# Five changes of stage worked in halves of 256 tokens instead of 512

## The reference

```python
h = rms_norm(x) * (1.0 + sc1) + sh1
x = x + g1 * mixer(h)
h = rms_norm(x) * (1.0 + sc2) + sh2
x = x + g2 * conv_ffn(h, ffn_w_up[i], ffn_conv_w[i], ffn_conv_b[i], ffn_w_down[i])
...
return rms_norm(x) * final_norm_g        # end of the first block; the second starts with a norm of this
```

## Time and profile before

| | |
|---|---|
| median of 3 runs | 3052.89 us (3051.44 to 3061.59) |
| profiled execution, its own time | 3053.06 us |
| its span | 3051.2 us |
| PE busy | 2935.6 us, 96% |
| DVE busy | 1805.3 us, 59% |
| ACT busy | 1100.8 us, 36% |
| POOL busy | 408.3 us, 13% |
| mean granted clock of TensorE | 0.976 |

### The profile page before, as it was taken

The page is one execution under the profiler, slowest core; times in us unless marked ns, Lnnn a source line. Parts: engine busy times, 40 slices in busy tenths (PEclk is TensorE's granted clock), DMA queues, the critical chain, the costliest instruction groups (busy, mean ns, idle before and its releaser), DMA issues. The chain is left out here.

```text
span 3051.2 us, 37640 instructions
## 1 busy us (share of the span) xinstructions
PE 2935.6 (96%) x15078; PEld 2445.1 (80%) x15078; DVE 1805.3 (59%) x2518; ACT 1100.8 (36%) x1569; POOL 408.3 (13%) x390
## 2 busy tenths in 40 slices
PE   6999988999999999999999999999999999999999
PEld 5778767788878878888768878888998887778887
DVE  7456546766656566765646697665764437554443
ACT  3233224333332342324324332234553336442322
POOL 0100111686642100001000000000000103100000
PEclk9999999999999999999989999999999999999999
DMA  6444322455648455554414356653563431123332
GB/s 267 146 131 139 111 89 84 148 176 174 227 131 269 157 166 154 157 152 128 128 44 150 112 178 189 196 166 119 170 182 91 147 95 49 35 89 97 97 97 83
DMA packets 123310, 421.00 MB, mean 138 GB/s; under 512 B 21520, under 2 KB 21520, under 8 KB 122368
## 3 DMA queue, kind: packets, MB, share of 16 engines
q1 hardware_dynamic: 102096, 369.67, 38.6%
q0 software_dynamic: 11056, 41.95, 4.1%
q10 hardware_dynamic: 9984, 6.97, 0.7%
HBM read 401.31 MB, written 19.86 MB: 138 GB/s over the span
## 5 line engine op out<-in xcount | busy, mean ns | idle before, releaser
L121 DVE TENSOR_TENSOR wl<-raw,wh 128x1024 fp32r<-128x1024 f32 x506 | 659.0, 1303 | 556.6 <-ACT wh L118 533.0
L112 PE MATMUL bk<-HH,wh 128*128 128x512 f32 x2176 | 863.4, 397 | 22.6 <-DVE HL L133 13.4
L112 PE MATMUL bk<-HL,wh 128*128 128x512 f32 x2176 | 856.4, 394 | 0.0
L112 PE MATMUL bk<-HH,wl 128*128 128x512 f32 x2176 | 855.6, 393 | 0.0
L118 ACT ACTIVATE wh<-raw 128x1024 fp32r<-128x1024 f32 x506 | 531.1, 1051 | 434.1 <-PE bk L112 426.8
L112 PEld LDWEIGHTS bk<-HH,wh 128*128 128x128 f32 x2176 | 415.0, 191 | 116.2 <-DVE HL L133 15.7
L112 PEld LDWEIGHTS bk<-HH,wl 128*128 128x128 f32 x2176 | 414.2, 190 | 88.0
L112 PEld LDWEIGHTS bk<-HL,wh 128*128 128x128 f32 x2176 | 414.7, 191 | 86.5 <-issue 1.0
L124 DVE CUSTOM_DVE_ANT_0 ttr<-ar,cB 128x1024 f32<-128x1024 f32 x240 | 309.1, 1288 | 2.2
L112 PE MATMUL bk<-gh,wh 128*128 128x512 f32 x704 | 275.4, 391 | 6.0 <-DVE glE L121 5.4
L112 PE MATMUL bk<-gh,wl 128*128 128x512 f32 x704 | 274.6, 390 | 0.0
(11 more groups left out here) (301 smaller groups left out, 3869.4 us busy)
## 6 DMA issues: line engine op xcount, KB each, us to landing
raw<-in_wts_dram SPq DMA_DIRECT2D x506, 512.0 KB, 3.6
ar<-in_ada_dram SPq DMA_DIRECT2D x176, 512.0 KB, 4.3
first<-in_ada_dram SPq DMA_DIRECT2D x16, 512.0 KB, 15.3
F_d<-CA POOLq DMA_DIRECT2D x8, 512.0 KB, 5.3
E_d<-stg POOLq DMA_DIRECT2D x16, 256.0 KB, 4.4
M_d<-K_d POOLq DMA_DIRECT2D x8, 512.0 KB, 11.5
EB<-E_d POOLq DMA_DIRECT2D x8, 512.0 KB, 5.9
EB<-M_d POOLq DMA_DIRECT2D x8, 512.0 KB, 7.3
```

The costliest lines, as they stand in the source:

```text
L112: return Nothing() if self.e is None else self.e.matmul(*a, **k)
L121: return Nothing() if self.e is None else self.e.tensor_tensor(*a, **k)
```

## The change

At the five changes of stage the work is done for tokens 0 to 255 and then for tokens 256 to 511.

- The last output tiles before the change (tiles 5 to 7; 4 to 7 behind retention; both products of tile 7 in glu) are made by `gemm_tail`: first the left halves of all of them, then the right halves. All three weight buffers stay in use until the right half of each is through.
- `half_sum` and `half_turn` for the left half are put between right halves of the tail on PE. Their counterparts for the right half are put into the first pair, behind blocks 2 and 6 of its left half (`pair_between`).
- `first_pair` makes the next stage's first two tiles, the left half over all 8 blocks and then the right half.
- DVE, ACT and POOL do their 512-wide operations as two of 256 (`halves_vec`, `halves_act`, `norm_adds`). The splits of the next stage's first two units, which stood among the additions to X before, now stand behind the first reciprocal and behind the first low half.
- At the change of blocks the two roots one after another become one for the even norm, of the sum of both statistics; the root and reciprocal for the first block's own norm come later.
- f1 and f3 read buffers of their own (`HH1`, `HL1`); the loads of the Fourier matrices on POOL's queue, which lie on the same memory, wait for f1's last up product; two points of `KNOTS` move; the exponential of the s5 tables on ACT comes behind the norm of f0.

```diff
+        def first_pair(e, tag, w0, n_out, xh, xl, xw, banks, frees, between):
+
+            u0 = open_units(tag, w0, n_out)
+            for hf in range(2):
+                for k in range(8):
+                    xw(e, k, hf)
+                    c = slice(k * 128, k * 128 + 128)
+                    for m in range(2):
+                        u, b = u0 + m, BK[banks[m]][:, 256 * hf:256 * hf + 256]
+                        if k == 0 and hf == 0:
+                            claim(e, banks[m])
+                            e.wait_ge(*act.of(("hi", u)))
+                            e.wait_ge(*vec.of(("lo", u)))
+                        h, lo = wh[u % NH][:, c], wl[u % NH][:, c]
+                        e.matmul(b, h, xh(k, hf), start=(k == 0), stop=False)
+                        e.matmul(b, h, xl(k, hf), start=False, stop=False)
+                        mm = e.matmul(b, lo, xh(k, hf), start=False, stop=(k == 7))
+                        if k == 7 and hf == 1:
+                            mm.then_inc(*pe.up(("unit", u), (tag, m)))
+                            bank[banks[m]] = frees(m)
+                    between(hf, k)
+            return u0
...
+        def gemm_tail(e, tag, u0, n_out, nk, cut, xh, xl, xw, banks, frees):
+
+            for hf in range(2):
+                n = cut * nk
+                for m in range(cut, n_out):
+                    bi = banks[m % len(banks)]
+                    b = BK[bi][:, 256 * hf:256 * hf + 256]
+                    claim(e, bi)
+                    for k in range(nk):
+                        u, pos = u0 + n // 8, n % 8
+                        n += 1
+                        if hf == 0:
+                            e.wait_ge(*act.of(("hi", u)))
+                            e.wait_ge(*vec.of(("lo", u)))
+                        xw(e, k)
+                        c = slice(pos * 128, pos * 128 + 128)
+                        h, lo = wh[u % NH][:, c], wl[u % NH][:, c]
+                        e.matmul(b, h, xh(k, hf), start=(k == 0), stop=False)
+                        e.matmul(b, h, xl(k, hf), start=False, stop=False)
+                        mm = e.matmul(b, lo, xh(k, hf), start=False, stop=(k == nk - 1))
+                        names = []
+                        if hf == 1 and (pos == 7 or n == n_out * nk):
+                            names.append(("unit", u))
+                        if k == nk - 1:
+                            names.append((tag, m, hf))
+                        if names:
+                            mm.then_inc(*pe.up(*names))
+                        if k < nk - 1:
+                            yield (m, hf, k)
+                    bank[bi] = frees(m, hf)
+                    yield (m, hf)
...
-        KNOTS = ((0, 0), (2, 16), (12, 24), (58, 48), (76, 48), (122, 78), (138, 78), (152, 88), (212, 124), (222, 124), (240, 136), (260, 136), (318, 192), (600, 192))
+        KNOTS = ((0, 0), (2, 16), (12, 24), (58, 48), (76, 48), (122, 78), (138, 78), (150, 88), (160, 88), (212, 124), (222, 124), (240, 136), (260, 136), (318, 192), (600, 192))
...
+        def half_sum(e, n, hf):
+
+            claim(e, 7)
+            w = con("one1024")[:, 0:1]
+            e.wait_ge(*pool.of(("ss", n.tag, 5) + (of_half(hf) if n.cut <= 5 else ())))
+            token_sums(e, 7, n.ssq[:, part(n, hf)], w, True, False, 2 * hf)
+            for j in (6, 7):
+                e.wait_ge(*act.of(squared(n, j, hf)))
+                mm = token_sums(e, 7, n.tm[j % 2][:, part(n, hf)], w, False, j == 7, 2 * hf)
+            mm.then_inc(*pe.up(("ms", n.tag, hf)))
+            bank[7] = (act, ("root", n.tag, hf))
...
+        def half_turn(e, n, hf):
+
+            b = n.banks[hf]
+            claim(e, b)
+            e.wait_ge(*vec.of(("rs", n.tag, hf)))
+            spread(e, b, n.st[:, 2 * hf:2 * hf + 2], 2).then_inc(*pe.up(("turned", n.tag, hf)))
+            bank[b] = (vec, ("xs", n.tag, 7, hf))
...
+        def halves_vec(e, n, added, split_first, split_next, inverse):
+
+            inverse(0)
+            split_first()
+            added(6)
+            norm_scaled(e, n, 0, 0)
+            norm_scaled(e, n, 1, 0)
+            norm_low(e, n, 0, 0)
+            split_next()
+            added(7)
+            for j in range(1, 8):
+                if j < 7:
+                    norm_scaled(e, n, j + 1, 0)
+                norm_low(e, n, j, 0)
+                if j == 4:
+                    inverse(1)
+            norm_scaled(e, n, 0, 1)
+            for j in range(8):
+                if j < 7:
+                    norm_scaled(e, n, j + 1, 1)
+                norm_low(e, n, j, 1)
+
+        def halves_act(e, n, square, split_next, root):
+
+            root(0)
+            square(6)
+            split_next()
+            norm_high(e, n, 0, 0)
+            norm_high(e, n, 1, 0)
+            square(7)
+            for j in range(2, 8):
+                norm_high(e, n, j, 0)
+                if j == 4:
+                    root(1)
+            for j in range(8):
+                norm_high(e, n, j, 1)
+
+        def pair_between(e, sums, turns):
+
+            def between(hf, k):
+                if (hf, k) == (0, 2):
+                    sums(1)
+                if (hf, k) == (0, 6):
+                    turns(1)
+            return between
...
+        def enter_vec(e, n, tag, x_ms, x_part, u):
+
+            need_mod(e, n.ms, n.parts[0])
+            need_mod(e, n.ms, n.parts[1])
+            halves_vec(e, n, lambda m: add_to(e, tag, m, m % 4, X, L, x_ms, x_part, 1), lambda: lo(e, u), lambda: lo(e, u + 1),
+                       lambda hf: half_inverse(e, n, hf))
...
+                if tail:
+                    for at_ in gemm_tail(e, tag, u0, 8, n, 5, lambda k, hf: half(f.gh, k, hf), lambda k, hf: half(f.gl, k, hf), xw, [0, 1, 2, 3],
+                                         lambda m, hf: (vec, ("x", tag, m, hf))):
+                        if at_ == (5, 1):
+                            f.halves.sum(e, 0)
+                        if at_ == (6, 1):
+                            f.halves.turn(e, 0)
...
+        HH1, HL1 = at("HH1", Z + 32768, [P, 8, L], R), at("HL1", Z + 49152, [P, 8, L], R)
+        n_f1 = norm("f1", X, L, HH1, HL1, 1, (3, 4), [], cut=7)
...
+            def inverse(hf):
+                st = n_e.st[:, 2 * hf:2 * hf + 2]
+                e.wait_ge(*pe.of(("ms", "fin", hf)))
+                e.tensor_scalar(st, BK[7][:, 2 * hf:2 * hf + 2], EPS, EPS, ALU.add, ALU.mult).then_inc(*vec.up())
+                e.wait_ge(*vec.now())
+                e.tensor_tensor(st, st, BK[7][:, 4 + 2 * hf:6 + 2 * hf], ALU.add).then_inc(*vec.up(("again", hf)))
+                half_inverse(e, n_e, hf)
...
             fence(e, "s5")
+            e.wait_ge(*pe.of((("f1", "up", NF - 1), 1)))
             e.dma_start(v_x.dl[:, :, :, :], d["dft512"]).then_inc(*d_dl["e"].up("dft"))
```

425 lines of the change are left out of this document (281 added, 144 removed).

## The result

The changed kernel took 3071.8 us (median of 5 runs, 3068.6 to 3079.9), the kernel before 3054.5 us (5 runs, 3051.4 to 3061.6): ratio 1.0052, 95% interval 1.0038 to 1.0066. It is slower, by more than the 0.3% that the prediction took for what a measurement can tell. The forecast was 3060 us with a range of 3046 to 3068: the way was right, slower, but the time lies above the range, on the side that had a chance of 0.39.

What follows compares the result with a forecast made beforehand. PE, busy for 96% of the span, was taken as the bound, with 53.2 us to win at the five changes. 3053.1 + 3.7 (windows) + 3.5 (half clock) = 3060 us, range 3046 to 3068.

Steps and rivals of the forecast that it cites:

- the side that had a chance of 0.39: Whole kernel slower by more than 0.3%, above 3062.0 us; chance 0.39.
- foreseen without clock: Five windows, tail's place to 49th matmul, before any clock term: together 111.3 against 107.57 us, +3.7.
- The array and the chain to the first HL: At each change, first HL matmul starts 2.65 to 4.25 us behind the tail's place; fifth 2.95 against 6.95.
- the fourth rival: At the changes, late ACT splits or POOL sums leave the first HL where it was: +4 each, 3077 us; chance 0.05.
- DVE's halves: In the pair, DVE sets the pace: 0.90 us per half block, both halves 1.80 against 1.45 us.
- the fastest rival: In the pair, queued 256-wide DVE operations cost half of 512-wide, 0.72 us a block: 3044 us; chance 0.12.
- I take three of five, +3.5: At the changes, early half-clock stretches of 3.4 us cost 1.0 to 1.3 us each; three of five assumed, +3.5.
- 6.5 as the upper bound: Clock term if each of the five changes has one early half-clock stretch: +6.5 us.
- rival (2): Half clock through most of the left half makes PE the pace, some +3 us at each change: 3068 us; chance 0.25.
- one hole of 2.3 us: Place in the earlier trace where the clock stood at 0.50 for 3.4 us behind a 2.3 us hole.
- Nothing for KNOTS: The `KNOTS` edit moves DVE work by a few units where PE does not wait; costed at nothing.
- The main claim: Over the five changes, some 25 us won ahead of the first HL are given back behind it: +3.7 us.

Runs made afterwards that it cites:

- the filled kernel: Changed kernel with 21 idle matmuls of 256 columns at each change, where PE would only wait: 3067.3 us, ratio 1.0032 to the kernel before.
- changed again: The changed kernel run once more without any edit, for a second profile: 3078.4 us in one run.
- divided sums: Changed kernel with idle matmuls, right half's turn one block earlier, and twin sums in six groups of four instead of 24 in a row: 3060.9 us, ratio 1.0018.
- the earlier turn: Changed kernel with the right half's turn behind block 5 instead of 6 and its first scaled tile ahead of the left's last low part: 3065.5 us, ratio 1.0029.
- third split ahead: Kernel with idle matmuls, earlier turn and divided twin sums, plus the third unit split before the pair's end, no idle matmuls behind the pair: ratio 1.0005.
- unfilled: Kernels in halves that have no idle matmuls in PE's waits at the changes of stage, among them the changed kernel at 3071.8 us.

## Why the prediction was wrong

The windows in one table, us. "Full clock" is from the filled kernel, whose DVE and ACT work is the changed kernel's:

| change | before | foreseen without clock | full clock | changed | changed again |
|---|---|---|---|---|---|
| 1 | 21.9 | 23.25 | 23.6 | 24.9 | 27.7 |
| 2 | 20.8 | 20.75 | 21.2 | 25.3 | 25.4 |
| 3 | 21.6 | 21.7 | 22.15 | 26.2 | 24.9 |
| 4 | 23.9 | 24.55 | not seen | 28.6 | 30.2 |
| 5 | 19.3 | 21.05 | 21.5 | 21.6 | 21.55 |

Against the forecast the profiled execution (3073.8 us) is 13.8 us over: 9.6 from the clock, 2.2 from the length of the windows at full clock, 1.7 from what lies between the windows, and the rest rounding.

**The array and the chain to the first HL: right.** Foreseen 3.6, 2.65, 2.8, 4.25 and 2.95 us, found 3.6, 2.7, 2.9, 4.4 and 3.1 (in the second profile 5.9 at the fourth). The tail's early statistics bring it forward by 3.8 to 6.7 us, as the steps said; the fourth rival is out.

**DVE's halves: right in kind, slightly small.** The four windows that were seen at full clock are 88.5 us together where the steps gave 86.75, 0.4 us more each. DVE's timeline in the fifth right half, in answer to the earlier trace rows (start, us):

```profile
2711.77 0.48 DVE L133 SCALAR_TENSOR_TENSOR HL<-tm,mods,HH 128x256 fp32r<-128x256 f32 x1 [0.18 <-ACT HH L118]
2712.29 0.48 DVE L133 SCALAR_TENSOR_TENSOR tm<-X,mods,bk 128x256 f32<-128x256 f32 x1
2712.69 0.48 DVE L133 SCALAR_TENSOR_TENSOR HL<-tm,mods,HH 128x256 fp32r<-128x256 f32 x1
2713.20 0.48 DVE L133 SCALAR_TENSOR_TENSOR tm<-X,mods,bk 128x256 f32<-128x256 f32 x1
2713.60 0.48 DVE L133 SCALAR_TENSOR_TENSOR HL<-tm,mods,HH 128x256 fp32r<-128x256 f32 x1
```

From one scaled tile to the next 0.91 us where 0.90 was taken; the fastest rival needed 0.80 or less. The estimate of 0.85 by the Trainium skill's page "VectorE: DVE Perf Modes", section "The TRN2 errata", was 0.06 too low. PE waits once for `wl` behind each pair, 0.4 to 2.4 us, as foreseen.

**The clock: the step that failed.** The prediction said: "I take three of five, +3.5", with 1.0 to 1.3 us for an early stretch. Three of five had a long stretch in the left half in the first profile, four in the second, but these lasted 10.2 us (one 6.8) and not 3.4: they begin some 3 us behind the first HL matmul and go on to the end of the left half. Each of 10.2 us cost 4.1 us (change 2: 25.3 against 21.2; change 3: 26.2 against 22.15). With some 25 us for the fourth at full clock (an estimate: the foreseen 24.55 and 0.4 as at the others), the clock's share in the first profile is 126.6 - 113.5 = 13 us, in the second 129.8 - 113.5 = 16, against 3.5 taken and 6.5 as the upper bound. (At full clock with divided sums the fourth window was 26.5 us, so the estimate for it may be up to 1.5 too low, and the clock's share then as much smaller.) This was rival (2), "the array stays at half clock through most of the left half"; it had 0.25. Its sum has a slip: 3060 with 15 more and the 3.5 less is 3071.5, and the text has 3068, the 3.5 taken off twice. Put right, it names the measured 3071.8, but partly by luck: it took 3 us at each of five changes, where the clock cost 4.1 at two, 1.2 at the first and nothing at the fifth, and halves and mixers made up the rest. It also left the doubling of the sums (1.2 us, 2.4 at the fourth) at "some more". The length could have been read before: the earlier trace rows give a mean clock of 0.77 over 21.91 us, which is 2 x 0.23 x 21.91 = 10.1 us at half clock, and likewise 6.7, 10.4, 10.0 and 7.0 for the others. The step took its 3.4 us from the earlier trace rows, one hole of 2.3 us, instead.

**What the same clock cost the old windows was missed too.** They had more of it, 44 us against 34, but half of that, 22.5 us, lay ahead of the first HL matmul, largely on waits for the chain. The other 22 us lay on the pairs and cost 9 us: with idle matmuls in the kernel before, whose pairs are at full clock, the stretch from the first HL matmul to the 49th takes 56.9 us over the five changes in place of 65.9. (The first HL came 4.1 us later in sum there, so the windows gained 5.) In the changed kernel all 34 us lie behind the first HL and cost 13. In both kernels that is some 0.4 us for each us of half clock on a pair; the change took waits out, and the half clock came to lie over work.

**Between the windows.** The remaining 1.7 us of the 20.7 were put at nothing. Ahead of the first change the half clock in retention ended 2 us earlier (-0.9). From the first change to the second the kernel takes 391.7 us in place of 392.5 (-0.9), as PE waits less for DVE's splits (PE's waits of the 50 us behind the pair, changed, then before; the same operation was waited for):

```profile
PE bk L112 <- DVE wl L121: 4.5, 3, 2.8
```

```profile
PE bk L112 <- DVE wl L121: 5.8, 2, 3.4
```

In the second profile that stretch takes 393.2 us, so this is no fixed effect of the change. The mixers behind changes 2 and 4 gave +2.1 and +1.3. Of the first, windows that begin 5.64 us apart, before and changed:

```profile
947.00:1010.00 63.00, 56.69 (x617) 51.82 (x613) 42.25 (x59) 20.30 (x31) 15.73 (x24) 0.86 0.69 238
```

```profile
952.64:1015.64 63.00, 57.96 (x611) 53.55 (x611) 40.64 (x58) 20.14 (x30) 15.72 (x24) 0.81 0.68 231
```

The mean clock is 0.81 in place of 0.86 with nearly the same work on DVE, 23.9 us of half clock in place of 17.1. Over all profiles this goes mostly with the change: eight of the nine profiles in halves have 23.9 us or more there, four of the five in full width 20.5 or less. And the clock is not all of it: the filled kernel has 17.1 us of half clock and its mixer still takes 175.3 us, as long as the changed kernel's, against 173.3 before. So some 2 us go with the change behind the second window, and why stays open. Behind the fourth the changed kernel has less half clock than the kernel before (64.9 against 68.3 us) and is 1.3 us longer; that is within what the profiles scatter by, and its cause is open too.

**Nothing for KNOTS.** With the old table the third window's chain is 0.9 us later, so the edit is worth up to 1 us rather than nothing, on its own good side.

**The main claim** ("what is won ahead of the first HL is given back behind it") stands against the kernel before as it ran: 25 us are won ahead, and behind it the full-clock pairs take some 31 us more, +6 where +3.7 was forecast. Part of what makes that so near is that the old pairs ran partly at half clock; against pairs at full clock the change gives back some 40 us for its 25. With filled holes, divided sums and the earlier turn the change still costs 0.2% (1.0006 to 1.0030) at full clock in all five windows, with the earlier turn's 0.8 us at four of them already taken off; only with the third split ahead as well can it no longer be told from the kernel before. So the direction, slower, came from the halves, as forecast; the clock decided the size.

## What to carry to other kernels

A hole that is cut up is not a hole that is gone: where PE works in short pieces between waits of 0.2 to 1.3 us, or through rows of one-column matmuls, ask whether the half clock now falls on work instead of on waiting, and read its likely length from the mean clock of the same place before. Compare with the old kernel's work at full clock as well, or its own half clock flatters the change. Idle matmuls in the waits are cheap to try (here 0.2% for nothing else changed), and sums divided into groups between matmuls with work in them served as well. Halving the width of operations of an engine that paces a pair costs it: 0.91 us for each half of a block, 1.82 together, against 1.45 for the whole.

## What the runs showed of the hardware

With a wait of 0.35 us more on PE ahead of one matmul, the fifth change had 6.8 us of half clock (1.2 in place of 2.4 GHz) where the other four unfilled profiles had none (0.38 us of delay on DVE became 3.1 us in the window). That is one profile and no threshold: the second change has such holes too (0.2, 0.6 and 0.5 us) and had the half clock in three of five. In the five unfilled profiles of the change 12 of the 15 windows of changes 1 to 3 had half clock, in the four filled ones none of 12. No wait of PE ahead of these stretches, within the change, was longer than 1.3 us. Behind 24 one-column sums in a row it came in two profiles with no wait at all. The same program gets it at other places in other executions (a stretch in retention began at 438.8 and at 440.1 us in two of the changed kernel), and the second window is 21.2 us long or 25.3 by that alone. The Trainium skill, page "TensorE: Matmul & The Clock Gate", Part 1, says that the same kernel shows a different number of slow matmuls at its start from run to run. The traces show the like at the changes of stage (3.4 and 10.2 us of half clock in the first window of the same kernel). The page adds that the penalty of that ramp is under 1% of a typical kernel's span and that a model should not be fitted to one count of slow matmuls. The half clock at the changes is not that ramp, but it too is under 1% here, 13 to 16 us of 3072, and it was most of the difference.

One-column matmuls with new weights each take 0.105 us at full and 0.20 us at half clock (12 of them in 1.26 and 2.42 us): they are not a fixed cost beside the clock.
